# Loading parameters from ScalarE's queue and moving the gMLP projection ahead, among the transposes

## The reference, cut to what matters

```
mod = silu(c) @ ada_w + ada_b            # 1024 -> 6144, one row for c_ctx, one for c
sh1, sc1, gt1, sh2, sc2, gt2 = split(mod, 6)
h = rmsnorm(x, norm1_g) * (1 + sc1) + sh1
p = h @ w_in                             # 1024 -> 1920 (A) + 512 (B) + 512 (C)
pa, pb, pc = split(p)
A: token shift, low-rank terms, RWKV-7 scan forward and backward
B: u, vg = split(gelu(pb)); layernorm(vg); 128x128 spatial matrix; u * (...)      # gMLP
C: a, b = split(pc); depthwise conv of a * sigmoid(b), 31 taps                    # conv module
x = x + gt1 * (concat(A, B, C) @ w_out)
h = rmsnorm(x, norm2_g) * (1 + sc2) + sh2
x = x + gt2 * moe(h)                     # 16 experts, grouped top 2
y = rmsnorm(x, final_g)
```

## Time and profile before

| | |
|---|---|
| median of 3 runs | 963.86 us |
| lowest and highest of them | 961.89 and 965.35 us |
| span of the profiled execution | 959.4 us |
| its own device time | not listed apart from the span |
| TensorE matmul busy | 792.3 us, 83% |
| VectorE busy | 501.5 us, 52% |
| ScalarE busy | 264.3 us, 28% |
| GpSimd busy | 141.4 us, 15% |
| mean granted TensorE clock | 0.907 |

### The profile page before, as it was taken

One profiled execution on the slowest core, in us unless ns is written; L12 is line 12 of the kernel. 1 busy time (PEld: TensorE's weight loads), 2 busy tenths in 40 slices (PEclk: granted clock), 3 DMA queues, 4 the chain that ended last, 5 costly groups with the idle time before them and its releaser, 6 DMA issues. The chain is left out here.

```text
span 959.4 us, 18027 instructions
## 1 busy us (share of the span) xinstructions
PE 792.3 (83%) x7510; PEld 491.9 (51%) x7510; DVE 501.5 (52%) x1052; ACT 264.3 (28%) x561; POOL 141.4 (15%) x136
## 2 busy tenths in 40 slices
PE   3699999999991749879889989998179999999930
PEld 3455455656551437767677864456144444444410
DVE  1310049973336899988989665342713333333322
ACT  2411013134243364746552721121010000000003
POOL 4000000000014120311200000000033333333120
PEclk9799999999996769979899999997579999999975
DMA  7962044072220000100000086213179999999655
GB/s 278 386 206 88 0 176 175 1 264 88 92 77 1 1 1 3 30 3 2 9 4 9 3 319 226 87 44 110 38 292 372 360 360 360 351 354 354 203 111 219
DMA packets 42345, 145.32 MB, mean 151 GB/s; under 512 B 6015, under 2 KB 8582, under 8 KB 37382
## 3 DMA queue, kind: packets, MB, share of 16 engines
q0 software_dynamic: 10368, 75.50, 23.0%
q1 hardware_dynamic: 31894, 68.63, 20.0%
HBM read 125.22 MB, written 19.43 MB: 151 GB/s over the span
## 5 line engine op out<-in xcount | busy, mean ns | idle before, releaser
L2242 PE MATMUL banks<-arena 128*128 128x512 f32 x304 | 157.1, 599 | 0.0
L1768 PE MATMUL banks<-arena 128*128 128x512 f32 x288 | 128.6, 600 | 1.1 <-ACT arena L1392 1.1
L2241 PEld LDWEIGHTS banks<-arena 128*128 128x128 f32 x304 | 57.0, 191 | 72.1 <-issue 69.6
L1768 PEld LDWEIGHTS banks<-arena 128*128 128x128 f32 x288 | 55.3, 193 | 70.7 <-issue 69.1
L1791 PE MATMUL banks<-arena 128*128 128x512 f32 x144 | 65.1, 595 | 1.6 <-DVEq L1208 1.6
L1640 DVE TENSOR_TENSOR arena<-arena,banks 128x256 f32<-128x256 f32 x18 | 7.6, 421 | 110.8 <-ACT arena L1398 105.0
L582 POOL TENSOR_TENSOR arena<-arena 128x640 f32<-128x640 f32 x8 | 13.7, 1723 | 329.1 <-DVE arena L759 329.1
L2241 PE MATMUL banks<-arena 128*128 128x128 f32 x304 | 60.0, 279 | 1.9 <-ACT arena L209 1.9
L2116 DVE TENSOR_TENSOR arena<-arena 128x641 f32<-128x641 f32 x15 | 12.4, 825 | 84.6 <-ACT arena L1975 84.6
L1398 ACT ACTIVATE arena<-banks 128x256 f32<-128x256 f32 x18 | 6.9, 385 | 179.9 <-PE banks L1768 179.9
L815 DVE TENSOR_TENSOR arena<-arena 128x30 f32<-128x30 f32 (+14 forms) x120 | 49.7, 414 | 4.1
(11 more groups left out here) (347 smaller groups left out, 1465.4 us busy)
## 6 DMA issues: line engine op xcount, KB each, us to landing
arena<-in_ada_w_dram SPq DMA_DIRECT2D x12, 2048.0 KB, 11.3
arena<-in_w_in_dram SPq DMA_DIRECT2D x5, 2048.0 KB, 15.0
arena<-modulations SPq DMA_DIRECT2D x8, 512.0 KB, 8.0
sum_rows<-arena SPq DMA_DIRECT2D x5, 512.0 KB, 2.6
h_rows<-arena SPq DMA_DIRECT2D x5, 512.0 KB, 3.6
arena<-sum_rows SPq DMA_DIRECT2D x5, 512.0 KB, 6.2
out_dram<-arena SPq DMA_DIRECT2D x5, 512.0 KB, 2.7
arena<-in_x_sample_dram SPq DMA_DIRECT2D x4, 512.0 KB, 7.6
```

The lines of the kernel that those rows point to most:

```text
L1768: x = T_.matmul(ps[2 + s][:, :], hT[:, s, c, :], wgu[:, s, c, :], start=(c == 0), stop=(c == KD - 1))
L2241: T_.matmul(ctx_[:, 0:P], w, h1T[:, k, 0:P], start=(k == 0), stop=(k == KD - 1))
L2242: x = T_.matmul(lat[:, :], w, h1T[:, k, P:T], start=(k == 0), stop=(k == KD - 1))
```

## The change

The 13 parameter transfers are issued by ScalarE, at the head of its stream, and no longer by SyncE. SyncE begins with x tile 0, `ada_w` block 0 and `ada_b`, then x tile 1, the spatial matrices, `ada_w` blocks 1 and 2, x tiles 2 and 3, block 3, x tile 4. Chunk 4 (gMLP) comes before chunk 5 (conv module) in `CHUNKS` and in `RING`. TensorE does only `xn_T(2)` ahead of the projections; each token tile t of chunk 4 waits for its own `h1T`, and `xn_T(t + 3)` follows it while there is one. ScalarE makes gelu 0 after `h1_act` of tile 3, gelu 1 after that of tile 4, and the other three behind them.

```diff
-        CHUNKS = [5, 4, 3, 1, 0, 2]
+        CHUNKS = [4, 5, 3, 1, 0, 2]
...
-        RING = [("ada", j) for j in range(4)] + [("proj", 5), ("proj", 4), ("ada", 4), ("proj", 3), ("ada", 5), ("proj", 1),
+        RING = [("ada", j) for j in range(4)] + [("proj", 4), ("proj", 5), ("ada", 4), ("proj", 3), ("ada", 5), ("proj", 1),
...
         @block.sync
         def _(sp):
-            def rows(name, ap):
-                s, n = PR[name]
-                sp.dma_start(prow[s:s + n, :], ap).then_inc(*up16("params_landed"))
...
-            rows("c_ctx", A["c_ctx"].rearrange("(r p) -> r p", p=P))
-            rows("c", A["c"].rearrange("o (r p) -> (o r) p", p=P))
...
-            rows("gmlp_bs", A["gmlp_bs"].rearrange("o g p -> (o g) p"))
-            sp.dma_start(crow, A["conv_w"].rearrange("o k (r p) -> (o k r) p", p=P)).then_inc(*up16("params_landed"))
             x_load(0)
+            ring_load(0)
+            sp.dma_start(adab, A["ada_b"][0].rearrange("(j g q) -> g j q", j=12, g=4)).then_inc(*up16("ada_b_landed"))
             x_load(1)
             sp.dma_start(wsrow, A["gmlp_ws"][0].rearrange("g p q -> p g q")).then_inc(*up16("ws_landed"))
-            sp.dma_start(adab, A["ada_b"][0].rearrange("(j g q) -> g j q", j=12, g=4)).then_inc(*up16("ada_b_landed"))
-            ring_load(0)
             ring_load(1)
+            ring_load(2)
             x_load(2)
             x_load(3)
-            ring_load(2)
             ring_load(3)
             x_load(4)
...
         @block.scalar
         def _(act):
             a = nc.scalar
+
+            def rows(name, ap):
+                s, n = PR[name]
+                act.dma_start(prow[s:s + n, :], ap).then_inc(*up16("params_landed"))
+
+            rows("c_ctx", A["c_ctx"].rearrange("(r p) -> r p", p=P))
...
+            act.dma_start(crow, A["conv_w"].rearrange("o k (r p) -> (o k r) p", p=P)).then_inc(*up16("params_landed"))
             act.wait_ge(*at("pcol"))
...
+            def gelu(t):
+                act.wait_ge(*at("proj_B", t))
+                a.activation(gl[:, t, :], ps[2 + t % 2][:, :], ACT.Gelu_apprx_tanh).then_inc(*up("gelu", t))
+
             for t in range(NT):
                 h1_act(act, t)
+                if t >= NT - 2:
+                    gelu(t - 3)
+            for t in range(2, NT):
+                gelu(t)
...
                     if m == 3:
-                        for t in range(NT):
-                            act.wait_ge(*at("proj_B", t))
-                            a.activation(gl[:, t, :], ps[2 + t % 2][:, :], ACT.Gelu_apprx_tanh).then_inc(*up("gelu", t))
                         act.wait_ge(*at("pad_zero"))
                         act.wait_ge(*at("conv_glu"))
...
-            for t in range(2, NT):
-                xn_T(t)
-            pe.wait_ge(*at("h1T_act", (NT - 1, 0)))
-            pe.wait_ge(*at("h1T_dve", (NT - 1, 1)))
+            xn_T(2)
...
                 if c == 4:
                     for t in range(NT):
+                        pe.wait_ge(*at("h1T_act", (t, 0)))
+                        pe.wait_ge(*at("h1T_dve", (t, 1)))
                         if t >= 2:
                             pe.wait_ge(*at("gelu", t - 2))
                         for k in range(KD):
                             x = T_.matmul(ps[2 + t % 2][:, :], h1T[:, k, t * P:(t + 1) * P], wslot(n)[:, k, :],
                                           start=(k == 0), stop=(k == KD - 1))
                         x.then_inc(*up("proj_B", t))
+                        if t + 3 < NT:
+                            xn_T(t + 3)
                     continue
```

More of the change, by code:

```diff
@@ L1926, in _ @@
             a = nc.scalar
+            def rows(name, ap):
+                s, n = PR[name]
+                act.dma_start(prow[s:s + n, :], ap).then_inc(*up16("params_landed"))
+            rows("c_ctx", A["c_ctx"].rearrange("(r p) -> r p", p=P))
+            rows("c", A["c"].rearrange("o (r p) -> (o r) p", p=P))
+            rows("norm1", A["norm1_g"].rearrange("o (r p) -> (o r) p", p=P))
+            rows("norm2", A["norm2_g"].rearrange("o (r p) -> (o r) p", p=P))
+            rows("mu", A["mu_shift"].rearrange("o (r p) -> (o r) p", p=P))
+            for n in ("w0", "a0", "k_k", "k_a"):
+                rows(n, A[n].rearrange("o d (r p) -> (o d r) p", p=P))
+            rows("r_k", A["r_k"].rearrange("o (r h) c -> (o r) (h c)", h=2))
+            rows("conv_b", A["conv_b"].rearrange("o (r p) -> (o r) p", p=P))
+            rows("gmlp_bs", A["gmlp_bs"].rearrange("o g p -> (o g) p"))
+            act.dma_start(crow, A["conv_w"].rearrange("o k (r p) -> (o k r) p", p=P)).then_inc(*up16("params_landed"))
             act.wait_ge(*at("pcol"))
```

## The result

The changed kernel takes 953.51 us, median of four runs (950.63 to 954.93), against 964.44 us for the kernel before, median of four (961.89 to 965.35). The ratio is 0.990, with a 95% interval of 0.987 to 0.993. One execution of the kernel before that took 3419 us in a later comparison is disturbed and left out of every figure.

The account below looks back on a forecast made before the run. TensorE, gapless from 60 us, was held at the start by `ada_w` blocks from a late-starting load stream, then by the wait for `h1T`. Terms 4.2 + 4.35 - 3.44 + 1.0 = 6.1 us gave 957.8 us, range 955.2 to 963.2.

Parts of the forecast that it names:

- The sum: At `ada_mm(4)`, start of part A: 4.2 + 4.35 - 3.44 + 1.0 = 6.1 us earlier, passed on to the end.
- block 3 earlier by 4.2: Load stream at the start: begun sooner without the parameters, it lands `ada_w` block 3 4.2 us earlier (bounds 2.5 and 4.6).
- from block 3 to the first product 4.35: Between modulation and projections: starting after one tile of `h1T` cuts 12.97 us to 8.6, a gain of 4.35.
- the median of the runs lies 4.5 above the profiled span, so 963.9: Base of the forecast time: median of the kernel before, 963.9 us, from which 6.1 was taken to give 957.8.
- eight transposes are 16 instructions; warm, two tiles took 3.44 us: TensorE's x transposes: 1.72 us a tile, 2.2 for `xn_T(2)` before the first product, 3.44 for two inside the projections.
- 0.7 lost: Token tile 0 of the first projection: low clock costs 0.7 us instead of 2.0; gain taken as 1.0.
- Rival 1: Start: bulk transfers hold back the parameters on ScalarE's queue, opening a hole before block 3; 963.2 us, chance 0.12.
- Waits among the token tiles: Chunk 4's projections: tiles 2 and 3 wait for gelus, covered by the tiles before; cost 0, uncovered 3.4 us.
- the conv product: VectorE, after the last `conv_gate`: delays ScalarE's copy of the `ada_mm(4)` row by 2 us, covered by part A; cost 0.
- Rival 3: Behind the projections: a later wait independent of them swallows the earlier start; 963 to 964 us, chance 0.06.
- Rival 2: Start: the bulk stream is served whole before ScalarE's queue, parameters at about 24 us; 966.2 us, chance 0.07.
- rival 4: Projections: the first weight block late or gelu waits of 3.4 us in two tiles lose 2 to 4 us; 960 to 962, chance 0.10.

Follow-up runs that it names:

- new_front: Changed kernel with x tiles 0 and 1 ahead of the parameter waits, block 3 ahead of x tile 2, first `w_in` block ahead of x tiles 3 and 4: 951.14 us.
- after: The changed kernel itself, in its first profile: span 953.2 us, median of four runs 953.51 us.
- params_doubled: Changed kernel with 13 further 8-row transfers on ScalarE's queue ahead of the parameters: ratio 0.996 to the kernel before.
- early_x: Changed kernel with squares, normalisation and transposes of x tiles 0 and 1 ahead of the waits for parameters and spatial matrices, loads in the same order: ratio 0.9905 to before.
- before_again: The kernel before, unaltered, profiled a second time: VectorE's first neighbour sum of part A at 129.8 us.

## Why the prediction was right or wrong, point by point

**The sum.** Forecast 6.1 us at `ada_mm(4)`; the pair of first profiles shows 8.2, the means of six and four profiles 6.2. By terms, forecast and means: block 3 earlier by 4.2, measured 3.8; from block 3 to the first product 4.35, measured 5.0; longer from there to the end of part C by 3.44 - 1.0 = 2.4, measured 2.6. The mechanism is the one that was forecast, and on the means its sum is too. In the first pair the stretch up to the first product shrank by 5.9, 1.6 more than forecast, and the stretch behind it grew by 1.7 only; that the means come out at the forecast's 6.2 is in part luck, since the first profile of before, from which every term was read, lay 2.0 us behind its mean at `ada_mm(4)`.

**What failed first is the base, "the median of the runs lies 4.5 above the profiled span, so 963.9".** The forecast time hangs on a median of three runs, and over 69 runs the kernel before has 961.9; from there the same 6.1 us would have given 955.8. Of the 4.3 us between 957.8 and 953.5, 2.0 are that; 0.9 is the changed kernel's four runs against its 954.4 over 21; 1.4 is the difference of 7.5 and 6.1. The term for it in the range, "some 1.5 for the median of runs", was too small: single runs of before cover 11 us. So the step that failed is the base and the width given to it, not the account of the gain.

**Mis-sized: "eight transposes are 16 instructions; warm, two tiles took 3.44 us".** The 16 recorded instructions were both tiles' together, 0.215 us for each transpose, and that was not warm throughout: it is nearer to the 0.25 us (1.97 for eight) that `new_front` shows where its window reads 0.50 than to the 0.13 inside the projections. There a tile takes 1.04 us, and `xn_T(2)` held the first product back by 0.91 (39.00 to 39.91) where I had 2.2. So two tiles inside cost 2.1 and not 3.44. **Mis-sized the other way: "0.7 lost" to the clock in token tile 0.** It took 8.56 us (39.91 to 48.47) against 6.87 for the others: 1.7 lost, against 2.0 before, so the gain from the clock was 0.3 in this pair and not 1.0. A window of that stretch, after:

```profile
41.00:42.00 1.00, 1.00 (x2) 0.33 (x1) 1.00 (x4) 0.65 (x2) 0.00 (x0) 0.50 1.04 387
```

**Rival 1** happened in its first half: the parameters came at 13.9 and the spatial matrices with them. The slack of 2.9 us, given for a T of 12.7, was used up to 1.0, and x tile 4's was used up altogether in one profile of four. Its costly form, more than a us for each transfer, did not occur; the other, a packet of the stream for each, is nearer to what the packet counts show, but the rows of the last transfer and the late begin of the queue were not in it. Doubling the transfers made the hole that the rival described, about a us for each us of delay beyond the 1.0 of slack: 4.55 later, 3.4 lost.

**Waits among the token tiles, the conv product, SyncE's later blocks:** at no cost, as said. **Rival 3** is not seen: the front's gain is there at the end within the scatter of the tail. **Rival 2 and rival 4** did not occur, apart from the 1.72 us wait for `w_in` in one profile, which is a part of rival 4.

## What to carry to other kernels

A stream of loads that runs at its full rate is worth only what its start and its holes are worth: count the bytes ahead of the block that is waited for, and for each gated issue the time at which the backlog runs dry. Small transfers on a second queue beside such a stream came 8.4 us after their last issue and not 2.5, so if a later load is gated by them, count that delay against its slack. And before a forecast of half a per cent, measure how far single runs of the kernel lie apart: one profile and three runs can each be 2 us off their mean.

## What the runs showed of the hardware that was not expected

Transfers of 1 to 31 KB on ScalarE's queue, beside SyncE's bulk, were waited for until 8.1 to 8.9 us after the last issue, 8.37 both with 13 (`after`) and with 26 (`params_doubled`), against 2.53 us on SyncE's queue with no bulk transfer ahead. Their packets went between those of the bulk, not behind them.

The granted clock in the windows can't be trusted at the start. In `early_x` the same 64 instructions took 3.59 and 1.93 us, in windows that both show 1.00:

```profile
18.67 3.59 PE L267 MATMUL banks<-arena 128*2 128x128 f32 x64
...
22.73 1.93 PE L267 MATMUL banks<-arena 128*2 128x128 f32 x64
```

```profile
18.00:20.00 2.00, 2.00 (x31) 1.39 (x34) 0.92 (x4) 0.00 (x0) 0.00 (x0) 1.00 1.05 390
20.00:22.00 2.00, 2.00 (x44) 1.25 (x36) 0.00 (x0) 0.00 (x0) 0.00 (x0) 1.00 1.04 385
22.00:24.00 2.00, 2.00 (x58) 1.64 (x54) 0.29 (x1) 0.00 (x0) 0.00 (x0) 1.00 1.05 404
```

The first recorded lower level in `before_again` is in the window from 28 to 30 us (0.68).

And identical code behind `ada_mm(4)` took 835.6 to 844.4 us from profile to profile (835.6 in `early_x`), at mean clocks of 0.89 to 0.91 over the span; no edit goes with it.
